# Two units in place of four run tile by tile at the end of the first out-projection

## The reference, cut to what matters

```python
# layer_a, last lines
out = jnp.concatenate([a_out, m_out], axis=-1) @ w_out      # 640x2048 @ 2048x2048
x1 = x + rms_norm(out, g_post)
# shared_kv
kv = rms_norm(x1, g_kv) @ w_kv                               # 640x2048 @ 2048x3072
```

## Time and profile before

| | |
|---|---|
| median of 3 runs | 2210.3 us (2210.18 to 2211.77) |
| profiled execution, first to last instruction | 2209.4 us |
| its PE, DVE, ACT, POOL busy | 98%, 52%, 40%, 15% |
| granted TensorE clock, share of full | 0.999 |
| PE waiting at the hand-over | 6.9 us |

### The profile page before, as it was taken

How to read it: one execution, slowest core, us unless ns; L and a number is a source line. 1 busy time by engine, 2 the same in 40 slices (tenths; PEclk the granted TensorE clock), 3 DMA queues, 4 the chain that set the end, 5 groups by cost and what they waited for, 6 DMA issues and landing times.

```text
span 2209.4 us, 33759 instructions
## 1 busy us (share of the span) xinstructions
PE 2170.8 (98%) x12524; PEld 1859.0 (84%) x12524; DVE 1144.3 (52%) x1970; ACT 883.2 (40%) x1701; POOL 321.1 (15%) x476
## 2 busy tenths in 40 slices
PE   8999999999999999999899999999999999999998
PEld 6788888888888998888788888888888888988887
DVE  5659889898744454224522222255555554663223
ACT  4543332333355343223422222456565654542221
POOL 1621202211101000002100000123131312010000
PEclk9999999999999999999999999999999999999999
DMA  7733434443744334222433333444444445544224
GB/s 268 238 88 111 113 107 112 114 108 107 230 132 161 107 109 171 77 76 100 157 100 100 116 105 103 132 139 138 138 149 143 135 144 186 167 152 171 77 76 152
DMA packets 177398, 293.38 MB, mean 133 GB/s; under 512 B 25476, under 2 KB 105008, under 8 KB 174000
## 3 DMA queue, kind: packets, MB, share of 16 engines
q1 hardware_dynamic: 133872, 164.57, 23.6%
q0 software_dynamic: 24448, 87.68, 12.7%
q10 hardware_dynamic: 19008, 40.18, 5.3%
HBM read 243.09 MB, written 48.61 MB: 132 GB/s over the span
## 4 chain that ended last, share of the span: by engine, by line
PE 71%; issue 12%; DVE 11%; ACT 3%; DMA 2%; POOL 1%; ACTq 0%; DVEq 0%; SPq 0%; POOLq 0%
PE PS L209 9%; PE PS L210 9%; PE PS L211 9%; PE PS L1542 9%; PE PS L1543 9%; PE PS L1544 9%; DVE WL L191 2%; PE PS L1504 2%; PE PS L1506 2%; PE PS L1505 2%; PE PS L823 1%; DVE FA L654 1%; DVE FA L650 1%; DVE FA L645 1%; DVE FA L647 1%
## 5 line engine op out<-in xcount | busy, mean ns | idle before, releaser
L209 PE MATMUL PS<-XH,WH 128*128 128x512 f32 (+1 forms) x1408 | 522.4, 371 | 1.1 <-DVE EST L2270 1.1
L191 DVE SCALAR_TENSOR_TENSOR WL<-RAW,vec,WH 128x256 fp32r<-128x256 f32 (+1 forms) x608 | 281.3, 523 | 461.6 <-ACT WH L177 457.1
L210 PE MATMUL PS<-XL,WH 128*128 128x512 f32 (+1 forms) x1408 | 511.1, 363 | 0.0
L211 PE MATMUL PS<-XH,WL 128*128 128x512 f32 (+1 forms) x1408 | 510.4, 363 | 0.0
L1542 PE MATMUL PS<-WH,XH 128*128 128x512 f32 x1168 | 457.0, 391 | 10.9 <-DVE WL L191 6.9
L1543 PE MATMUL PS<-WL,XH 128*128 128x512 f32 x1168 | 455.2, 390 | 0.0
L1544 PE MATMUL PS<-WH,XL 128*128 128x512 f32 x1168 | 455.1, 390 | 0.0
L177 ACT ACTIVATE WH<-RAW,vec 128x256 fp32r<-128x256 f32 (+1 forms) x608 | 281.8, 534 | 340.8 <-DMA RAW<-in_w_kv_dram 172.3
L186 DVE TENSOR_TENSOR WL<-RAW,WH 128x1024 fp32r<-128x1024 f32 (+1 forms) x120 | 143.8, 1204 | 322.7 <-ACT WH L173 322.5
L211 PEld LDWEIGHTS PS<-XH,WL 128*128 128x128 f32 x1408 | 264.4, 188 | 38.1
L209 PEld LDWEIGHTS PS<-XH,WH 128*128 128x128 f32 x1408 | 264.9, 188 | 35.0 <-issue 1.8
(11 more groups left out here) (326 smaller groups left out, 2388.6 us busy)
## 6 DMA issues: line engine op xcount, KB each, us to landing
RAW<-in_w_in_a_dram SPq DMA_DIRECT2D x64, 512.0 KB, 4.1
RAW<-in_w_in_b_dram SPq DMA_DIRECT2D x64, 512.0 KB, 3.9
RAW<-in_w_kv_dram SPq DMA_DIRECT2D x48, 512.0 KB, 3.6
RAW<-in_w_out_a_dram SPq DMA_DIRECT2D x32, 512.0 KB, 3.4
RAW<-in_w_out_b_dram SPq DMA_DIRECT2D x32, 512.0 KB, 3.4
scratch_in_a<-EST ACTq DMA_DIRECT2D x32, 320.0 KB, 3.9
RAW<-in_w_glu_dram SPq DMA_DIRECT2D x24, 384.0 KB, 3.2
scratch_in_b<-EST ACTq DMA_DIRECT2D x26, 320.0 KB, 3.5
```

The lines of the kernel that those rows point to most:

```text
L191: ins = eng.scalar_tensor_tensor(out=wview(WL, slot, ph)[:, kt, :], in0=wview(RAW, slot, ph)[:, kt, :], scalar=vec[:, g:g + 1], in1=wview( ...
L209: pe.matmul(acc, wh, xh, start=first, stop=False)
L210: pe.matmul(acc, wh, xl, start=False, stop=False)
L211: return pe.matmul(acc, wl, xh, start=False, stop=last)
```

## The change

The last chunk of the first out-projection (`out_a`) keeps two units, 6 and 7, for the run tile by tile, and runs six units over all tiles. With that the buffers of units 4 and 5 come free earlier, and key units 0 and 1 can be loaded, and split by ACT and DVE, ahead of the tiles' chains. No transposes stand between the tiles any more; they and the key units' runs get another order on PE, and ACT, DVE and POOL get other orders. The second out-projection (`out_b`) keeps its order.

```diff
-            def last_chunk(ph, then=None):
+            def last_chunk(ph, held, then=None):
 ...
-                for k in range(RING):
+                begun = ph.upc - held
+                for k in range(begun):
                     unit_moving(pe, ph, U + k, k, n, NT)
 ...
-                for t in range(2):
-                    units(t, RING, ph.upc - 1)
+                early = 2 if held == RING else 0
+                for t in range(early):
+                    units(t, begun, ph.upc - 1)
                 for t in range(NT):
-                    units(t, ph.upc - 1 if t < 2 else RING, ph.upc)
+                    units(t, ph.upc - 1 if t < early else begun, ph.upc)
 ...
-            def x1_between(t):
-                if t >= 3:
-                    turn_x1(pe, t - 3)
-            last_chunk(phases["out_a"], x1_between)
+            last_chunk(phases["out_a"], 2)
 ...
-            for t in range(2):
-                for k in range(2):
-                    kv_unit(k, (t,))
-                turn_x1(pe, t + 2)
-            for k in range(3):
-                kv_unit(k, (2,))
-            kv_unit(2, (0, 1))
-            for k in range(3):
-                kv_unit(k, (3,))
-            turn_x1(pe, NT - 1)
-            kv_unit(3, (0, 1))
-            for k in range(3):
-                kv_unit(k, (NT - 1,))
-            kv_unit(3, (2, 3, 4))
+            turn_x1(pe, 0)
+            turn_x1(pe, 1)
+            kv_units(0, 2, 0)
+            turn_x1(pe, 2)
+            kv_units(0, 2, 1)
+            kv_units(2, 4, 0)
+            kv_units(2, 4, 1)
+            turn_x1(pe, 3)
+            kv_units(0, 4, 2)
+            turn_x1(pe, 4)
+            kv_units(0, 4, 3)
+            kv_units(0, 4, 4)
```

More of the change, by code:

```diff
@@ L1748, in _, with kv_units @@
             row_chunks(phases["out_a"], (F_A, ORDER_A), lambda t: pe.wait_ge(s_ev["glu"], 21 + min(t, 3)), last=1)
-            def x1_between(t):
-                if t >= 3:
-                    turn_x1(pe, t - 3)
             def x1_copied(t):
                 pe.wait_ge(s_xl, 28 + 4 * t + 4)
-            last_chunk(phases["out_a"], x1_between)
+            last_chunk(phases["out_a"], 2)
             ph = phases["kv"]
-            def kv_unit(k, only):
-                unit_moving(pe, ph, ph.first + k, k, 0, NT, ready=x1_copied if k == 0 else None, only=only)
-            for t in range(2):
-                for k in range(2):
-                    kv_unit(k, (t,))
-                turn_x1(pe, t + 2)
-            for k in range(3):
-                kv_unit(k, (2,))
-            kv_unit(2, (0, 1))
-            for k in range(3):
-                kv_unit(k, (3,))
-            turn_x1(pe, NT - 1)
-            kv_unit(3, (0, 1))
-            for k in range(3):
-                kv_unit(k, (NT - 1,))
-            kv_unit(3, (2, 3, 4))
+            def kv_units(first, end, t):
+                for k in range(first, end):
+                    unit_moving(pe, ph, ph.first + k, k, 0, NT, ready=x1_copied if k == 0 else None, only=(t,))
+            turn_x1(pe, 0)
[10 more added lines that the diff above has]
+            kv_units(0, 4, 4)
             for k in range(4, ph.upc):
-                kv_unit(k, None)
+                unit_moving(pe, ph, ph.first + k, k, 0, NT)
             with pe.Fori(1, ph.chunks) as i:
@@ L1801, in _ @@
             row_chunks(phases["out_b"], (F_B, ORDER_B), lambda t: pe.wait_ge(s_ev["in_b"], 61 + min(t, 3)), last=1)
-            last_chunk(phases["out_b"])
+            last_chunk(phases["out_b"], RING)
         @block.scalar
@@ L1967, in _ @@
             out_rows_squared(0)
+            next_unit(0)
             out_square(0, 3, 0)
+            next_unit(1)
             out_square(0, 3, 1)
+            out_square(0, 3, 2)
             x1_squared(0)
-            out_square(0, 3, 2)
+            out_square(0, 3, 3)
             x1_squared(1)
-            out_square(0, 3, 3)
+            turned_high(act, 7)
+            out_square(0, 3, 4)
             x1_squared(2)
[L1975 to L1978, removed]
             turned_high(act, 8)
+            next_unit(2)
+            next_unit(3)
             x1_squared(3)
             turned_high(act, 9)
-            next_unit(2)
+            x1_squared(4)
             turned_high(act, 10)
-            x1_squared(4)
-            next_unit(3)
             turned_high(act, 11)
@@ L2202, in _ @@
             out_rows(0)
+            next_unit(0)
             out_row(0, 3, 0)
+            next_unit(1)
             out_row(0, 3, 1)
             residual(0, 0)
+            out_row(0, 3, 2)
             residual(0, 1)
-            out_row(0, 3, 2)
             normalised(0)
+            out_row(0, 3, 3)
             residual(0, 2)
             normalised(1)
-            out_row(0, 3, 3)
             turned_low(dve, 7)
+            out_row(0, 3, 4)
+            residual(0, 3)
             normalised(2)
-            residual(0, 3)
-            next_unit(0)
-            next_unit(1)
             turned_low(dve, 8)
-            out_row(0, 3, 4)
+            next_unit(2)
+            next_unit(3)
             normalised(3)
+            residual(0, 4)
             turned_low(dve, 9)
-            residual(0, 4)
-            next_unit(2)
+            normalised(4)
             turned_low(dve, 10)
-            normalised(4)
-            next_unit(3)
             turned_low(dve, 11)
@@ L2364, in _ @@
             x1_root(2)
-            x1_root(3)
             pool.wait_ge(s_xt, 32)
@@ L2368, in _ @@
             out_root(0, 4)
+            x1_root(3)
             x1_root(4)
```

## The result

| | before | changed |
|---|---|---|
| median of 20 runs each, side by side | 2212.4 us (2209.4 to 2215.4) | 2216.0 us (2212.0 to 2221.5) |
| ratio, with its 95% interval | 1 | 1.0015 (1.0010 to 1.0021) |
| profiled execution: span | 2209.4 us | 2211.3 us (its time: 2213.0) |
| PE waits, from 1018 us to unit 4's start | 6.9 us in 4 | 7.9 us in 3 |

The change costs 0.15%, some 3.3 us (0.0015 x 2212): inside the bound of 0.2% that the prediction set, on its slower side. The interval lies clear of 1, so the loss is real, and its upper end reaches that bound. The profiled execution alone shows 1.9 us more span, to 2211.3, where 2211.4 was forecast. So two things have to be explained: why the mechanism came out as foretold, and where the other 1.4 us go.

A forecast was written before the change was run, and what follows sets the result against it. PE, busy nearly throughout, was taken as the bound. Its idle time goes from 7.7 to about 10 us, unit 4 starts 1.9 later, plus 0.1: span 2211.4, with 0.9 around it 2212.3 us, range 2209.0 to 2217.0.

The forecast's parts named there:

- Tile 0's bank full at 1036.6, unit 1's low half from 1039.1: Out-projection's end: bank full after 72 matmuls in place of 42; unit 1's load, taken as 3.4 us, lets DVE begin.
- DVE's queue then decides: Hand-over: DVE's work from 1039.1 sums to 22.7 us, so tile 1's third low-half group ends at 1061.8.
- POOL isn't held: Rival, hand-over: without DVE's three waits 1.75 us come back, 2210.6 us; chance 0.10.
- PE's waits of 1.0 and 3.2 at tiles 0 and 1: Hand-over: PE idles 1.0 us until tile 0 is normalised at 1048.4, then 3.2 until tile 1 is at 1053.4.
- The release of unit 4: Behind the hand-over: unit 0 free 18 matmuls before the end, not 30; unit 4 waits 3.0 us, starts at 1093.4.
- The clock falls: Rival: PE drops to the lower clock behind the new 3.2 us idle stretch; costs 3.5 us, 2215.8; chance 0.12.
- The idle times of the sum: PE idles about 10 us in and behind the hand-over, where it idled 7.7 before.
- the way of unit 4's load: From unit 0 free at 1086.3: issue 0.35, load 3.90, ACT 1.37, DVE to PE 1.47, giving 1093.4.
- The 0.9 us around the span: Whole kernel: median of three timed runs, 2210.3 us, less the profiled span, 2209.4, carried over to the forecast.
- a late load: Rival, hand-over: unit 1's load takes 7.28 us, making all 3.9 us later, 2216.2; chance 0.12.
- no change: Whole kernel: the time stays within about 0.2%, 4.4 us, of the kernel before; chance 0.70.
- Tiles ahead of PE: Rival, hand-over: tiles keep ahead of PE, its idle time vanishes, unit 4 starts 5.4 us earlier, 2204.9; chance 0.06.

The follow-up runs named there:

- e6: Changed kernel plus one unused DVE pass ahead of unit 1's low half; unit 4 starts 71.03 us behind ACT's last out-projection high half, in place of 69.80.
- e7: Changed kernel with unit 1's halves moved later, the low half behind residual 1; unit 4 starts 69.75 us behind ACT's last out-projection high half, in place of 69.80.
- e2: Changed kernel with key unit 3 run last over tiles 2 to 4, freeing unit 0 earlier; ratio 0.9995 to the kernel before.
- e3: Changed kernel with 14 useless matmuls between the transposes of tiles 0 and 1, keeping PE busy; ratio 1.0011 to the kernel before.
- e5: Changed kernel with the edits of e2 and e3 together; ratio 0.9998 to the kernel before.
- e9: Changed kernel, unedited, profiled three more times; spans 2216.7, 2217.1 and 2214.7 us.
- e8: The interleaved order of e4 with key unit loads and x1 stores set apart, halves and tile 4's row load moved; ratio 0.9970 to the kernel before, 2205.0 us.
- e4: Changed kernel with units 4 to 7 interleaved over tiles, transposes between, unit 3's work last, other engines' orders matched; ratio 0.9981 to the kernel before.

## Why the prediction was right, point by point

- **Tile 0's bank full at 1036.6, unit 1's low half from 1039.1:** 1036.65 and 1039.36. The load took 3.90 us, not 3.4; less by the issue at 1034.06, it came 0.3 us late on DVE.
- **DVE's queue then decides:** the sum of 22.7 us, 1061.8, came out near 1062.1, and both waits for POOL of 0.73 are there, which rules out the rival "POOL isn't held". e6 shows the queue as the gate by itself. One sentence is too strong, that all later tiles queue behind unit 1's half: DVE would have waited for tile 1's bank in that time, and e7 moved the half at no cost. The sum was right since the two gates fall within half a microsecond.
- **PE's waits of 1.0 and 3.2 at tiles 0 and 1:** 1.4 and 3.8. Tile 1's transposes began at 1054.62, not 1053.4, since PE's transposes go in step with tile 0's low half (L1610 from 1053.79) and not with the normalising; nothing hung on it, as tile 2 was gated by DVE.
- **The release of unit 4, 3.0 us of wait at 1093.4:** 2.7, with 3.08 from matmul to matmul, at 1094.07. e2 takes that wait alone away, and the whole loss with it.
- **The clock falls:** the rival was priced at the wrong place. It fell at the hand-over, behind the longer stretch, but the 3.5 us weren't paid: matmuls there had slack up to tile 2's gate (e3 and e5, where the fall is gone, gain nothing). What the step left out is a fall *behind unit 4's wait*, where everything after hangs on PE. There it costs 1.6 us, in three of four profiled executions; of e3, e6 and e7, which have the same wait, only e3 shows it, so four of seven. Unit 4 itself starts 70.0 us behind the half in the mean of the four, and 67.2 in that of the two profiles of the kernel before: 2.8 later. With 0.9 to 1.2 for the fall (four of seven or three of four times 1.6) that makes 3.7 to 4.0, an estimate from few profiles, against 3.3 measured (2.2 to 4.6).
- **The time itself:** 2212.3 forecast, 2216.0 measured. Of the 3.7 us, 2.1 are the base: the kernel before has a median of 2212.4 over 20 runs, not the 2210.3 of three. The other 1.6 are of the size of that fall and of unit 4's start, forecast 69.3 us behind the half (1093.4 - 1024.1) and measured at 69.8 to 70.1. The idle times of the sum don't give its result: about 10 less 7.7 is more than 1.9. It was the way of unit 4's load that gave 1093.4, and that held. The 0.9 us around the span was mis-sized with it: I had set one execution's span against the median of others, and where both are known of one execution the difference is 1.7 (2212.98 - 2211.3 after, 2218.37 - 2216.7 in e9). In absolute time 2216.0 is where the rivals lay (2215.8 for the clock, 2216.2 for a late load), but not by their reasons. That "no change" held all the same is in part luck: a fall that the sum didn't have took up much of the room to 0.2%.
- **Tiles ahead of PE:** didn't happen, as the sum on DVE said. e8 shows what it takes: its two first turns begin at 1045.34 and 1048.00.

What stays open: why some executions show a fall behind unit 4's wait and others don't. The length of PE's idle stretch there doesn't tell: 2.69 us by the record in the first profile, 2.82 in e6 and 2.79 in e7 brought no fall, 2.73 to 2.95 in e9 and 2.79 in e3 did. Windows behind the wait in e6, then in e7:

```profile
1098.00:1100.00 2.00, 2.00 (x11) 1.63 (x10) 1.28 (x3) 1.80 (x3) 0.00 (x0) 1.00 0.17 58
1096.00:1098.00 2.00, 2.00 (x10) 1.66 (x9) 2.00 (x4) 1.74 (x3) 0.00 (x0) 1.00 0.04 8
```

## What to carry to other kernels

Before adding a reordering's gains, list for each buffer that is reused *behind* the reordered stretch how much work now stands between its last use and the next load's first use; here the earlier loads won nothing in the end (with the release put back, e2, unit 4 starts at 67.0, and at 67.4 and 67.0 in the kernel before), as the tiles came later for it, and 18 matmuls in place of 30 made a loss of it. Price an idle stretch of the engine by what hangs on the work right behind it: the same fall of the clock was free where another engine was the gate, and cost 1.6 us where PE was. And a clock's rows in one profile are one draw: look at several executions before a fall is called absent.

## What the runs showed of the hardware that was not expected

- The lower clock can come *after* work has begun again. In e9's first execution PE idled to 1095.24 and ran three matmuls, 0.34 and 0.23 us apart, before the spacing went to 0.43; in the other two the fall came 1.0 and 1.3 us behind the wait. It lasted 8 to 9 matmuls there. In e3 it lasted 13 and had come before the work, in a window in which PE did nothing:

```profile
1092.00:1094.00 2.00, 0.00 (x0) 0.00 (x0) 1.37 (x2) 0.86 (x2) 0.00 (x0) 0.85 0.94 334
```

  The Trainium skill (TensorE: Matmul & The Clock Gate, part 1) says that the lower level is the default and activity releases it. The traces agree in so far as the falls here follow idle stretches (2.73 to 2.95 us in e9) and end while PE is busy; stretches of 2.69 to 2.82 us without a fall (the changed kernel's first profile, e6, e7) that sentence alone doesn't explain.
- Normalising holds POOL as well as a residual does. POOL's first step under the residual at 1041.36 took 2.22 us and under the normalising at 1047.50 took 1.28, where it took 0.19 with DVE idle. The Trainium skill (GPSIMD Engine Reference, the table of specifications) names VectorE instructions with two inputs in SBUF, or in a 2-port performance mode, as what POOL contends with; the residual has two inputs. Which mode normalising runs in no row names; it passes the same 128x2048 elements in 1.29 us where the residual takes 2.34 (DVE, at 1047.50 and 1041.36). POOL's rows:

```profile
1038.22 0.19 POOL L1636 TENSOR_SCALAR rstd<-ss 128x1 f32<-128x1 f32 x1 [195.83 <-DVE ss L2165]
...
1041.53 2.22 POOL L1636 TENSOR_SCALAR rstd<-ss 128x1 f32<-128x1 f32 x1 [2.46 <-DVE ss L2165]
...
1047.55 1.28 POOL L1636 TENSOR_SCALAR rstd<-ss 128x1 f32<-128x1 f32 x1
```

- A weight load of 512 KB took 3.7 to 3.9 us in a quiet stretch and 8.81 among stores of x1 and the load of tile 4's rows (e4). How much of the difference between e4 and e8 is due to it isn't shown: e8 changes the orders of PE, ACT, DVE and POOL as well.
